# Three transformer blocks in split float32: the order of work on ScalarE and VectorE at the fourth norm, in the feed-forwards, at the end of the HGRN branch and in the gated branches, and the last rows by column halves

## The reference, cut to what matters

```python
for layer in range(2):                       # first block
    y = mlstm_mixer(rms_norm(x)) or stick_breaking_mixer(rms_norm(x))
    x = x + rms_norm(y)
    x = x + rms_norm(memory_cross_attention(rms_norm(x), mem_n, ...))
    x = x + rms_norm(swiglu_ffn(rms_norm(x), w_gate_up, w_down))
# second block
h = _rmsnorm(x, norm_mix_g); z = h @ w_in
y_a = _hgrn2_mixer(...); y_b = _fox_mixer(...); y_c = _memory_mixer(...)
merged = gates[0]*(y_a @ w_br_hgrn) + gates[1]*(y_b @ w_br_fox) + gates[2]*(y_c @ w_br_mem)
x = x + merged @ w_out
h2 = _rmsnorm(x); a, v = split(h2 @ w_up)    # 2816 columns each
x = x + (gelu(causal_conv3(a) + b) * v) @ w_down
```

## Time and profile before

| what | value |
|---|---|
| median of three runs | 1362.43 us (1361.47 to 1362.52) |
| the profiled execution | 1362.48 us, its span 1360.8 us |
| mean granted TensorE clock | 0.992 |
| PE busy | 1323.0 us (97%), 7353 matmuls |
| PEld busy | 1133.7 us (83%) |
| DVE, ACT, POOL busy | 861.6, 703.8, 105.5 us |
| DMA | 223.64 MB, 164 GB/s over the span |

### The profile page before, as it was taken

One profiled execution on the slowest core, in us unless ns is written; L12 is line 12 of the kernel. 1 busy time (PEld: TensorE's weight loads), 2 busy tenths in 40 slices (PEclk: granted clock), 3 DMA queues, 4 the chain that ended last, 5 costly groups with the idle time before them and its releaser, 6 DMA issues.

```text
span 1360.8 us, 17718 instructions
## 1 busy us (share of the span) xinstructions
PE 1323.0 (97%) x7353; PEld 1133.7 (83%) x7353; DVE 861.6 (63%) x992; ACT 703.8 (52%) x968; POOL 105.5 (8%) x173
## 2 busy tenths in 40 slices
PE   6999999999999999999999999999999999899998
PEld 6889897988888988779888888898777877778887
DVE  4466664766666644376576666767864565677776
ACT  4555554544444676754454444555554653544553
POOL 7000100100000100020100000101310002000000
PEclk9999999999999999989999999999999999999999
DMA  8644553555555543244365555544434444355552
GB/s 264 205 155 155 178 178 117 182 192 197 193 187 186 182 129 124 93 156 155 99 210 187 186 185 187 184 155 125 156 124 152 134 148 155 124 172 199 186 186 93
DMA packets 154785, 223.64 MB, mean 164 GB/s; under 512 B 6055, under 2 KB 106563, under 8 KB 154704
## 3 DMA queue, kind: packets, MB, share of 16 engines
q1 hardware_dynamic: 152912, 218.18, 48.2%
q0 software_dynamic: 1664, 4.27, 1.0%
q10 hardware_dynamic: 128, 0.05, 0.0%
HBM read 221.44 MB, written 1.05 MB: 164 GB/s over the span
## 4 chain that ended last, share of the span: by engine, by line
PE 83%; DVE 9%; ACT 5%; issue 2%; POOL 1%; DMA 1%; SPq 0%; POOLq 0%; DVEq 0%; ACTq 0%
PE ps L392 17%; PE ps L394 8%; PE ps L416 8%; PE ps L417 8%; PE ps L418 7%; PE ps L377 5%; PE ps L378 5%; PE ps L379 5%; PE ps L541 4%; PE ps L542 4%; PE ps L543 4%; DVE wlo L1529 4%; ACT whi L1038 2%; PE ps L441 1%; PE ps L468 1%
## 5 line engine op out<-in xcount | busy, mean ns | idle before, releaser
L1529 DVE TENSOR_TENSOR wlo<-raw,whi 128x1024 fp32r<-128x1024 f32 x412 | 498.4, 1230 | 333.1 <-ACT whi L1038 329.2
L1038 ACT ACTIVATE whi<-raw 128x1024 fp32r<-128x1024 f32 x412 | 423.5, 1050 | 286.7 <-PE ps L418 141.6
L392 PE MATMUL ps<-RR,whi 128*128 128x512 f32 x1056 | 367.3, 398 | 5.5 <-DVE ar L1649 2.9
L394 PE MATMUL ps<-RR,wlo 128*128 128x256 f32 x1056 | 274.1, 280 | 0.1
L416 PE MATMUL ps<-whi,RR 128*128 128x512 f32 x592 | 238.9, 404 | 5.1 <-DVE ar L2056 3.0
L417 PE MATMUL ps<-wlo,RR 128*128 128x512 f32 x592 | 232.2, 392 | 0.0
L418 PE MATMUL ps<-whi,RR 128*128 128x512 f32 x592 | 232.1, 392 | 0.0
L392 PEld LDWEIGHTS ps<-RR,whi 128*128 128x128 f32 x1056 | 191.9, 189 | 43.7 <-DVE ar L1649 3.6
L394 PEld LDWEIGHTS ps<-RR,wlo 128*128 128x128 f32 x1056 | 199.7, 189 | 12.5 <-DVE RR L1559 0.8
L377 PE MATMUL ps<-RR,whi 128*128 128x256 f32 x512 | 148.8, 291 | 7.4 <-DVE RR L1559 7.0
L378 PE MATMUL ps<-RR,whi 128*128 128x256 f32 x512 | 146.9, 287 | 0.0
(11 more groups left out here) (320 smaller groups left out, 1302.0 us busy)
## 6 DMA issues: line engine op xcount, KB each, us to landing
raw<-in_ffn_w_gate_up SPq DMA_DIRECT2D x44, 1024.0 KB, 5.0
raw<-in_ffn_w_down SPq DMA_DIRECT2D x33, 1024.0 KB, 4.9
raw<-in_w_in SPq DMA_DIRECT2D x28, 1024.0 KB, 5.0
raw<-in_ffn_w_up SPq DMA_DIRECT2D x22, 1024.0 KB, 5.0
raw<-in_xa_w_kv SPq DMA_DIRECT2D x16, 1024.0 KB, 5.2
raw<-in_ml_w_in SPq DMA_DIRECT2D x12, 1024.0 KB, 5.7
raw<-in_sb_w_qkv SPq DMA_DIRECT2D x12, 1024.0 KB, 5.1
raw<-in_xa_w_q SPq DMA_DIRECT2D x8, 1024.0 KB, 5.1
```

The costliest lines, as they stand in the source:

```text
L392: m = pe.matmul(two(ps[:, bank, :]), p.hi[:, k, :], XT2[:, k, :, :], start=k == 0, stop=k == 7)
L394: pe.matmul(ps[:, bank, 0:256], p.lo[:, k, :], X.h[:, k, :], start=False, stop=False)
L1038: act.activation(p.hi, p.raw, ACT.Copy).then_inc(S["w_hi"], 1)
L1529: dve.tensor_tensor(p.lo, p.raw, p.hi.bitcast(F32), ALU.subtract).then_inc(S["w_lo"], 1)
```

## The change

Each item moves instructions; no arithmetic is added or left out.

- Fourth norm. ACT makes two `whi` pieces before the squares of the memory rows. DVE makes two `wlo` pieces and the low parts of the norm first, and norms the memory rows last.
- Feed-forwards (all three). DVE sums the banks of g and of u before it makes the `wlo` pieces of that step, where it did so after them. In the third, ACT's Gelu stands behind the pieces of u.
- HGRN's end. ACT copies `A01` ahead of Exp, and squares the first 128 rows between Exp and Ln; the pieces of `past("fva")` come after the squares, on DVE after the products with the gate. DVE takes the first sum ahead of the forget gate's chain and the second behind it.
- Branches. PE puts the first tile of br10 ahead of the last output of the memory attention. br21 uses banks 1 and 3 in place of 0 and 1, and the first product with w_out no longer waits for br21's banks. DVE scales br21 ahead of the pieces of `past("br21a")`.
- Last rows. In the last step of the third feed-forward, PE finishes one PSUM bank after the other (rows t, column half), DVE adds 128x512 four times in place of 128x1024 twice, and SP writes four times 256 KB in place of twice 512 KB.

```diff
@@ feed_forward, PE
+                    if last and f == 2:
+                        for t in range(NT):
+                            for half in range(2):
+                                o, c = ps[:, 2 * t + half, :], slice(512 * half, 512 * half + 512)
+                                for i, p in enumerate(pp):
...
+                                m.then_inc(S["f_first"], 1)
+                        return
@@ branches, PE
-                if i >= 3:
+                if 3 <= i < 6:
                     outputs(2, i - 3, mv, 1)
             pe.wait_ge(S["mg0"], 1)
-            tm("br10a", Yb, 0, 4, (2, 3), ("mg0", 2))
+            tm_tile("br10a", Yb, 0, 4, 2, 0)
+            outputs(2, 3, mv, 1)
+            pe.wait_ge(S["mg0"], 2)
+            tm_tile("br10a", Yb, 0, 4, 3, 1)
...
-            pe.wait_ge(S["mt"], 3)
-            tm("br21a", Yc, 0, 4, (0, 1), ("mt", 4))
+            pe.wait_ge(S["mt"], 4)
+            tm("br21a", Yc, 0, 4, (1, 3), ("mt", 6))
             Xm = Rows(XTh, XTl, S["mT_lo"], [k + 1 for k in range(8)])
+            out_chunk("mo", 0, Xm)
+            turn(mg[:, :, 512:1024], 4, "mg", (7, 8), (4, 5, 6, 7), "mT_T", own=True)
             pe.wait_ge(S["mt"], 7)
-            out_chunk("mo", 0, Xm, ("mt", 5))
-            turn(mg[:, :, 512:1024], 4, "mg", (7, 8), (4, 5, 6, 7), "mT_T", own=True)
-            pe.wait_ge(S["mt"], 8)
-            out_chunk("mo", 1, Xm, ("mt", 6))
+            out_chunk("mo", 1, Xm, ("mt", 8))
@@ feed_forward, ACT
                     past(f"u{f}_{j}")
+                    if f == 2:
+                        conv_gelu(j)
@@ fourth norm, ACT
             squares(4)
+            past("V1_1a")
             mem_squares(1)
-            past("V1_1a")
@@ HGRN's end, ACT
-            act.wait_ge(*at("f_min", 1))
-            act.wait_ge(S["act_step"], step(act.activation(fc, fc, ACT.Exp)))
-            act.activation(fc, fc, ACT.Ln, bias=1.0).then_inc(S["f_ln"], 1)
             act.wait_ge(S["h_A01m"], 1)
             act.activation(A01.rearrange("p h t -> p (h t)"), ps[:, 4, :], ACT.Copy).then_inc(S["h_A01"], 1)
-            past("fva")
+            act.wait_ge(*at("f_min", 1))
+            f_exp = step(act.activation(fc, fc, ACT.Exp))
             for t in range(NT):
                 act.wait_ge(S["h_o"], t + 1)
                 act.activation(KQ[0][:, 512 * t:512 * t + 512], ps[:, 6 + t, :], ACT.Square).then_inc(S["ho_sq"], 1)
+                if t == 0:
+                    act.wait_ge(S["act_step"], f_exp)
+                    act.activation(fc, fc, ACT.Ln, bias=1.0).then_inc(S["f_ln"], 1)
+            past("fva")
@@ feed_forward, DVE
-                    past(f"g{f}_{j}")
                     dve.wait_ge(S["w_used"], end(f"g{f}_{j}"))
                     dve.tensor_reduce(two(f_sum[j % 2]), ...).then_inc(S["f_gate"], 1)
+                    past(f"g{f}_{j}")
...
-                    past(f"u{f}_{j}")
                     dve.wait_ge(S["w_used"], end(f"u{f}_{j}"))
                     dve.tensor_reduce(two(f_prod[j % 2]), ...).then_inc(S["f_up"], 1)
+                    past(f"u{f}_{j}")
@@ fourth norm, DVE
+            past("V1_1a")
+            norm_lo(4, gain1(1, 2))
+            first_tile(Vx[:, 0, 512:1024], "V1_1b", 6, "V_dve")
             mem_normed(1)
-            past("V1_1a")
-            first_tile(Vx[:, 0, 512:1024], "V1_1b", 6, "V_dve")
-            norm_lo(4, gain1(1, 2))
@@ branches, DVE
+            next_branch("br21a", 5, (1, 3), 3)
             past("br21a")
-            next_branch("br21a", 5, (0, 1), 3)
@@ last rows, DVE and SP
+            for t in range(NT):
+                for half in range(2):
+                    c = slice(512 * half, 512 * half + 512)
+                    dve.wait_ge(S["f_first"], 3 + 2 * t + half)
+                    dve.tensor_tensor(xr[:, t, c], xr[:, t, c], ps[:, 2 * t + half, :], ALU.add).then_inc(S["resid"], 1)
...
+                    sp.dma_start(o2[:, t, c], xr[:, t, c]).then_inc(S["out"], 16)
```

More of the change, by code:

```diff
@@ L40 @@
         ("lb_e", 1)),
-        "m2_act": (("mk_act", 1), ("mv_act", 1), ("h_ln", 1), ("hi_act", 1), ("fq_act", 1), ("fk_act", 1), ("f_ln",
-        1), ("h_A01", 1), ("fv_act", 1), ("mq_act", 1)),
+        "m2_act": (("mk_act", 1), ("mv_act", 1), ("h_ln", 1), ("hi_act", 1), ("fq_act", 1), ("fk_act", 1), ("h_A01",
+        1), ("f_ln", 1), ("fv_act", 1), ("mq_act", 1)),
         "m2_dve": (("mk_dve", 1), ("mv_dve", 1), ("h_k", 1), ("h_G", 1), ("hi_dve", 1), ("fq_dve", 1), ("fk_dve", 1),
@@ L533, in down @@
                     pp = C[f"d{f}_{j}"].pieces
+                    if last and f == 2:
+                        for t in range(NT):
+                            r = slice(128 * t, 128 * t + 128)
+                            for half in range(2):
+                                o, c = ps[:, 2 * t + half, :], slice(512 * half, 512 * half + 512)
+                                for i, p in enumerate(pp):
+                                    if not t and not half:
+                                        pe.wait_ge(S["w_lo"], p.n + 1)
+                                    pe.matmul(o, h[:, i, r], p.hi[:, 0, c], start=False, stop=False)
+                                    pe.matmul(o, h[:, i, r], p.lo[:, 0, c], start=False, stop=False)
+                                    m = pe.matmul(o, h[:, 2 + i, r], p.hi[:, 0, c], start=False, stop=i == 1)
+                                m.then_inc(S["f_first"], 1)
+                        return
                     for i, t in ([(0, 0), (1, 0), (0, 1), (1, 1)] if last else [(0, 0), (0, 1), (1, 0), (1, 1)]):
@@ L1144, in hidden, with conv_gelu @@
                     c.then_inc(S["f_tap2"], 1)
+                def conv_gelu(j):
+                    tmp = f_tmp[j % 2]
                     act.wait_ge(S["f_conv"], j + 1)
@@ L1582, in post_add @@
                                              ALU.add).then_inc(S["resid"], 1)
[L1584 to L1588, removed]
             def pair(dst, name, bank, sem):
@@ L1950, in vector_program @@
             dve.scalar_tensor_tensor(fc, fl, -1.0, fl, ALU.mult, ALU.min).then_inc(S["f_min"], 1)
+            head_scaled(0, "fq_n")
+            dve.wait_ge(S["ho_sq"], 1)
+            dve.tensor_reduce(ho_st[0][0], heads(KQ[0][:, 0:512], 4), AX.X, ALU.add).then_inc(S["ho_ss"], 1)
             dve.wait_ge(*at("f_ln", 1))
@@ L1955, in vector_program @@
             dve.tensor_scalar(fl, fc, -1.0, None, ALU.mult).then_inc(S["f_ng"], 1)
-            head_scaled(0, "fq_n")
-            past("fva")
-            for t in range(NT):
-                dve.wait_ge(S["ho_sq"], t + 1)
-                dve.tensor_reduce(ho_st[t][0], heads(KQ[0][:, 512 * t:512 * t + 512], 4), AX.X, ALU.add).then_inc(S["ho_ss"], 1)
-            head_sums(1)
+            dve.wait_ge(S["ho_sq"], 2)
+            dve.tensor_reduce(ho_st[1][0], heads(KQ[0][:, 512:1024], 4), AX.X, ALU.add).then_inc(S["ho_ss"], 1)
             for t in range(NT):
@@ L1969, in vector_program @@
                 dve.tensor_tensor(hg[:, t, :], hg[:, t, :], o, ALU.mult).then_inc(S["h_z"], 1)
+            past("fva")
+            head_sums(1)
             past("fvb")
@@ L2093, in vector_program @@
             feed_forward(2)
-            plain_add(("f_first", 3), ("w_used", end(f"d2_{NJ - 1}")))
+            for t in range(NT):
[3 more added lines that the diff above has]
+                    dve.tensor_tensor(xr[:, t, c], xr[:, t, c], ps[:, 2 * t + half, :], ALU.add).then_inc(S["resid"], 1)
         def gpsimd_program(pool):
@@ L2255, in sync_program @@
             for t in range(NT):
-                sp.wait_ge(S["resid"], 13 + t)
-                sp.dma_start(o2[:, t, :], xr[:, t, :]).then_inc(S["out"], 16)
-            sp.wait_ge(S["out"], 32)
+                for half in range(2):
+                    c = slice(512 * half, 512 * half + 512)
+                    sp.wait_ge(S["resid"], 13 + 2 * t + half)
+                    sp.dma_start(o2[:, t, c], xr[:, t, c]).then_inc(S["out"], 16)
+            sp.wait_ge(S["out"], 64)
         block = ctx.enter_context(nc.Block())
```

## The result

The changed kernel takes 1346.5 us, the median of four runs (1345.04 to 1346.86); the kernel before took 1361.95 in four runs beside it (1359.71 to 1362.52). The ratio is 0.9885 with a 95% interval of 0.9872 to 0.9899: faster by 15.5 us, where 18.7 were forecast (1343.8, range 1341.8 to 1347.6). The profiled execution took 1346.26 us, its span is 1344.5, 16.2 shorter than before.

The account below looks back on a forecast made before the run. PE bounds the kernel, busy 1323.0 of 1360.8 us. Gains of 5.9 + 5.1 + 0.2 + 6.4 + 1.1 = 18.7 us, off the profiled 1362.48, gave 1343.8 us, range 1341.8 to 1347.6.

Parts of the forecast that it names:

- rival 1: New waits, as at HGRN's end, pull the clock down for one or two stretches: 1345.5 to 1347.2 us; chance 17%.
- Fourth norm, 5.9: At the fourth norm, PE's wait for the low parts goes (3.3 us) and the clock stays up (2.6): 5.9 us gained.
- The clock part: Behind the fourth norm's wait, 27 matmuls return from 5.7 us to 3.2 at full rate: 2.6 us gained.
- Third feed-forward, 5.1: In the third feed-forward, PE's waits go since DVE's sum starts when PE is done: 5.1 us gained.
- the other two feed-forwards: In the first and second feed-forward, pieces behind the sums keep a margin of 3.1 us: cost 0.
- rival 2: The third feed-forward's waits come back in part, half of the 5.1 us stays: 1346.4 us; chance 8%.
- rival 4: Sums ahead of pieces make weights late in every step of all feed-forwards; slower than before, 1373.5 us; chance 2%.
- HGRN's end, 0.2: At HGRN's end, the A01 wait goes, waits of about 1.4 and 1.6 us come: 0.2 us gained.
- Rival 3: A drain behind the table load exists and HGRN's end loses 1.2 us: 1345.2 us; chance 4%.
- Branches, 6.4: At the branches, waits go for 1.7 and net 3.0 us, and a half-clock stretch for 1.7: 6.4 us gained.
- Last rows, 1.1: At the end, the smaller last add gains 0.53 us and the halved last transfer 0.6: 1.1 us.
- The low stretches: Sign over the whole kernel: the forecast is wrong if half-clock stretches are not fewer by two.

Follow-up runs that it names:

- e4: The changed kernel with the fourth norm put back as before: 1351.59 us, ratio 0.992 to the kernel before.
- e1: The changed kernel with the feed-forwards' order of before on DVE (sums behind pieces) and ACT (Gelu ahead of pieces): 1351.52 us, ratio 0.9919.
- e5: The changed kernel with only ACT's half of the feed-forward order put back (Gelu behind the convolution, ahead of the pieces): 1345.55 us, ratio 0.9883.
- e6: The changed kernel with only DVE's half of the feed-forward order put back (pieces ahead of sums): 1346.73 us, ratio 0.989.
- e2: The changed kernel with HGRN's end put back as before (Exp and Ln ahead of the copy of A01): 1344.49 us, ratio 0.9866.
- e7: The kernel before with only the change at HGRN's end put in: 1364.73 us, ratio 1.0018 to the kernel before.
- e3: The changed kernel with the branches put back as before: 1353.46 us, ratio 0.9928 to the kernel before.
- e10: The changed kernel with four adds of 128x512 kept but two transfers of 512 KB: one execution, 1346.7 us; 4.17 us from last matmul's start to the end.
- e8: The changed kernel with DVE's and ACT's order at HGRN's end changed again, sums, copies and keys ahead of pieces: 1341.98 us, ratio 0.9854.
- e9: The changed kernel with the last rows' matmul order, adds and transfers put back as before: one execution, 1347.27 us; 4.70 us from last matmul's start to the end.

## Why the prediction came out as it did

The time lies inside the forecast range, 2.7 us above the point, but not by the forecast's own account, which had 66%. What happened is rival 1, with 17%: new waits drew the clock down for one stretch, for which it gave 1345.5. The other 1.0 us matches the late start of this profile, for which no step had a term; that it fell within the range as well is luck. By its own steps:

- **Fourth norm, 5.9: right.** 5.92 in the profile; put back (e4), 5.1. The wait (3.3) is as forecast. The clock part is 2.6 only against the execution of before with its long stretch; in e4 it was half as long, and the place lost 4.6. I had read one execution's clock as fixed.
- **Third feed-forward, 5.1: right.** 5.07, and 5.0 in e1. The chain as told holds, but e5 and e6 show that either edit alone would have done nearly all of it. Nothing in the other two feed-forwards: right, their lengths differ by 0.04 at most. Rival 2, half of the waits coming back, is refuted; rival 4, late weights, too.
- **HGRN's end, 0.2: this step failed.** Its order and its waits were forecast to 0.1 us: 1.46 and 1.53, gain 0.04. What failed is that the sum gave these waits their length only and left the clock at full, although rival 1 named the very thing, with 17%. The runs show a stretch at half clock behind them in nine kernels of nine, 3.4 us in eight of them, 1.6 us of cost. So the part as a whole is a loss: 1.6 us at the place in e2 and 1.5 in e7 (2.0 and 2.9 in the medians, where the rest isn't located). The bound given for it (loss 1.4) was too narrow for the same reason. The prediction took waits of 1.33 and 1.53 that were followed by full clock as evidence. Behind the first there were only two of 0.6 and 0.7 within 10 us, the second stood alone, and the two new ones are both of 1.5 and stand 8 us apart; that this is the difference is argued, not shown.
- **Rival 3, a drain behind the load: refuted.** 0.01 us between load and Ln.
- **Branches, 6.4: right.** 6.32, and 6.3 at the place in e3. The two outer waits and the low stretch are gone. Their terms measured 1.72, 3.01 and 1.62 (forecast 1.7, 3.0, 1.7). The second tile of br21, which needs bank 3, came 0.26 us late, where 0.25 was set.
- **Last rows, 1.1: right.** 1.16, split 0.53 and 0.62 by e10, as forecast (0.53 and 0.6). The fixed 2.0 us that the prediction set beside its row is what the Trainium skill (DMA: Bandwidth & Descriptors, Anatomy of one DMA) fits to transfers issued by GpSimd; these are SyncE's, and the rows leave 1.4.
- **The low stretches.** The text said it would be wrong if they were not fewer by two. Two went, one came, so they are fewer by one: by its own test the forecast was wrong in that.
- **What the sum couldn't have.** 1.08 us of the profile's difference arises before 20 us, where nothing was changed, and 0.4 came back at the norm before the third feed-forward. The sum of the parts as forecast is 18.7 and as measured 18.5; less 1.6 and 1.1, plus 0.4, it is 16.2, the difference of the spans.

What stays open: why the same waits at the norm before the third feed-forward are followed by one stretch (seven kernels, before and after among them), by a double one (e2, e3, e8, e9) or by none (e4): with one profile of each, kernel and execution can't be told apart. The same holds for the double stretch of e6 at HGRN's end. Whether one of the two waits at HGRN's end would be enough for its stretch wasn't tried.

## What to carry to other kernels

On an in-order engine put what frees or feeds the busiest engine ahead of what prepares its later weights: at three places such an order took waits of 3.2, 2.4 and 3.0 us away (at the branches together with other banks), and at HGRN's end, where the change did not do it, e8 gained another 4.5. Price a wait of the matmul engine by its length plus the low clock that may stand behind it: here two new waits of 1.5 us cost more than the three of 1.3, 0.7 and 0.7 that they replaced. When two edits shorten one chain, try each alone, since one may be all that is needed.

## What the runs showed of the hardware

- Between 20 us and the last matmul, the low-clock stretches of all twelve profiled kernels lasted 3.4 or 6.8 us (windows at 0.50 or 0.51). At HGRN's end 3.4 cost 1.6 us, and 6.8 in e6 cost 3.1. Behind the same waits at the norm before the third feed-forward there was none, one of 3.4 or one of 6.8 from one profile to the next, and the time over that place differed by up to 1.9 us (e4 against e9). A clock part read from one profile is no surer than that.
- A low stretch can replace waits rather than add to them: in e1's third feed-forward it cost 1.5 us and 1.3 us of later delays were gone.
- A table load of 1.28 us was followed by Ln 0.01 us later, in both kernels.
- At 100 us the twelve profiles are up to 1.8 us apart (e6 0.3 early, e4 1.5 late, against the kernel before), with no edit there. How long PE stayed at half rate up to 20 us, and whether a stretch near 60 us lasted 3.4 us, 6.8 us or was missing, accounts for it.
- A last transfer of 256 KB landed 2.0 us after its issue and one of 512 KB after 2.6.
